# Softmax denominators of a dilated attention: summed over steps on GpSimd and over keys once a head on TensorE, output inverted and scaled in place

## What is computed

```python
def _dilated_pattern(qh, kh, vh, window, dilation):
    ...
    s = jnp.einsum('brnikge,brnjke->brnkgij', qs, kk)
    ...
    m = jnp.max(s, axis=-1)
    pexp = jnp.exp(s - m[..., None])
    l = jnp.sum(pexp, axis=-1)
    o = jnp.einsum('brnkgij,brnjke->brnikge', pexp, vv)

def dilated_attention(q, k, v, q_g, k_g):
    ...
    res = [_dilated_pattern(qh, kh, vh, w, d) for (w, d) in DILATED_PATTERNS]
    m_max = jnp.max(jnp.stack([r[1] for r in res]), axis=0)
    wts = [jnp.exp(r[1] - m_max) for r in res]
    num = sum(wi[..., None] * r[0] for wi, r in zip(wts, res))
    den = sum(wi * r[2] for wi, r in zip(wts, res))
    out = num / den[..., None]
```

## Time and profile before the change

| | us |
|---|---|
| median of 3 runs (3523.31 to 3527.47) | 3525.03 |
| the profiled execution | 3533.12 |
| its span, first to last instruction | 3531.4 |
| from the start of the mixers' transfers to the last store of that phase, about | 766 to 1408 |

### The profile page before, as it was taken

How to read it: one execution, slowest core, us unless ns; L and a number is a source line. 1 busy time by engine, 2 the same in 40 slices (tenths; PEclk the granted TensorE clock), 3 DMA queues, 4 the chain that set the end, 5 groups by cost and what they waited for, 6 DMA issues and landing times. The chain is left out here.

```text
span 3531.4 us, 38277 instructions
## 1 busy us (share of the span) xinstructions
PE 3181.3 (90%) x15558; PEld 2484.2 (70%) x15620; DVE 1606.5 (45%) x1490; ACT 813.0 (23%) x1136; POOL 329.4 (9%) x224
## 2 busy tenths in 40 slices
PE   5899999947989878799789999999998899997699
PEld 4678888824555545678568888888887787886587
DVE  5771145536466433532454444444444422422343
ACT  4221111112333433300221111111110421321331
POOL 4000000012333322000210000000000000000100
PEclk8899999968999989899889999999999999998899
DMA  3132222155385560642301111111111643532342
GB/s 120 66 130 67 71 69 73 59 141 152 98 211 139 147 156 32 197 147 97 132 36 48 48 48 48 48 48 48 48 48 37 233 165 108 194 122 81 125 133 67
DMA packets 222781, 356.21 MB, mean 101 GB/s; under 512 B 36993, under 2 KB 122241, under 8 KB 212417
## 3 DMA queue, kind: packets, MB, share of 16 engines
q1 hardware_dynamic: 218674, 333.71, 29.8%
q0 software_dynamic: 4000, 21.01, 1.6%
HBM read 257.45 MB, written 97.17 MB: 100 GB/s over the span
## 5 line engine op out<-in xcount | busy, mean ns | idle before, releaser
L78 PE MATMUL up_ps<-up_h_hi,up_w_hi 128*128 128x512 f32 x1408 | 555.7, 395 | 35.7 <-DVE up_h_lo L184 34.9
L79 PE MATMUL up_ps<-up_h_lo,up_w_hi 128*128 128x512 f32 x1408 | 553.0, 393 | 0.0
L80 PE MATMUL up_ps<-up_h_hi,up_w_lo 128*128 128x512 f32 x1408 | 552.4, 392 | 0.0
L78 PE MATMUL inp_ps<-inp_h_hi,inp_w_hi 128*128 128x512 f32 x896 | 358.5, 400 | 31.5 <-DVE inp_h_lo L184 28.7
L79 PE MATMUL inp_ps<-inp_h_lo,inp_w_hi 128*128 128x512 f32 x896 | 353.5, 394 | 0.0
L80 PE MATMUL inp_ps<-inp_h_hi,inp_w_lo 128*128 128x512 f32 x896 | 352.8, 394 | 0.0
L78 PEld LDWEIGHTS up_ps<-up_h_hi,up_w_hi 128*128 128x128 f32 x1408 | 267.3, 190 | 98.8 <-issue 32.7
L80 PEld LDWEIGHTS up_ps<-up_h_hi,up_w_lo 128*128 128x128 f32 x1408 | 267.5, 190 | 56.4
L79 PEld LDWEIGHTS up_ps<-up_h_lo,up_w_hi 128*128 128x128 f32 x1408 | 267.7, 190 | 55.7 <-issue 0.5
L78 PE MATMUL down_banks<-down_a_hi,down_w_hi 128*128 128x512 f32 x704 | 276.8, 393 | 29.5 <-DVE down_a_lo L1814 27.1
L1683 DVE TENSOR_TENSOR up_squares<-up_ps,up_rstd 128x2048 f32<-128x2048 f32 x44 | 100.9, 2292 | 440.8 <-PE up_ps L80 431.0
(11 more groups left out here) (274 smaller groups left out, 4867.0 us busy)
## 6 DMA issues: line engine op xcount, KB each, us to landing
down_a_raw<-act SPq DMA_DIRECT2D x14, 2816.0 KB, 12.2
act<-up_room SPq DMA_DIRECT2D x22, 1024.0 KB, 4.6
up_room<-in_w_up_dram SPq DMA_DIRECT2D x42, 512.0 KB, 5.9
mix_m_t<-cum_rows SPq DMA_DIRECT2D x16, 1024.0 KB, 5.5
inp_room<-in_w_in_dram SPq DMA_DIRECT2D x26, 512.0 KB, 5.0
xbc<-inp_room SPq DMA_DIRECT2D x12, 1024.0 KB, 4.6
mix_xbc<-xbc SPq DMA_DIRECT2D x16, 768.0 KB, 4.3
down_w_raw<-in_w_down_dram SPq DMA_DIRECT2D x44, 256.0 KB, 3.0
```

The lines of the kernel that those rows point to most:

```text
L78: pe.matmul(out, w_hi, x_hi, start=first, stop=False)
L79: pe.matmul(out, w_hi, x_lo, start=False, stop=False)
L80: return pe.matmul(out, w_lo, x_hi, start=False, stop=last)
```

## The change

- `values` no longer makes denominators. `add` works on half the columns; `o_den` becomes `o_sum`, outputs alone.
- GpSimd gets a new loop. For each head it clears `p_sum` (128 x 2 x 2048), and after each exponential adds that step's probabilities into the columns of `p_sum` that belong to their query tokens: dense for dilation 1, every 4th column for dilation 4, every 16th for dilation 16. Each add waits for the one before it. ScalarE may write a buffer of `probs` only when values and GpSimd are both done with what it held.
- After the last step, `sums` on TensorE multiplies `p_sum` by a tile of ones 64 wide, four blocks of 512 columns, each for two query heads side by side, into the four banks. It waits for all adds of GpSimd and VectorE. So each denominator stands on all 64 rows of its head's outputs. ScalarE copies each bank over the first half of `p_sum`.
- `divide` on VectorE inverts each block of 512 columns in place and multiplies `o_sum` by it. The store of `o_sum` follows when all four blocks are done (`sync_out`). The trip of the denominators through DRAM is gone, as are `den_rows` and its use in `out_projection`.
- The planned times: steps at k / (STEPS + 11), 8 units more between (2,2) and (2,3), the mixer's chunk at 26.4 units for 26.0. The next head's second loads stand right behind the last step.
- Waits that are new: the first pass of heads 2 and 3 and the second pass of heads 1 to 3 wait for ScalarE's copies of the sums of the head before; GpSimd's memset waits for the division of the head before.
- The row maxima are folded on 32 partitions of 128 columns, in 12 small transfers instead of 6.

```diff
     def in_step(self, r, k):
-        return self.at(2, r, k / (self.STEPS + 3))
+        return self.at(2, r, k / (self.STEPS + 11))
...
-            at += long[which - 1]
+            at += long[which - 1] + (8.0 if (which, r) == (2, KVH - 2) else 0.0)
...
-        def store(r):
-            sp.wait_ge(self.o_add, self.VALUES * (r + 1))
-            for n in range(4):
-                sp.dma_start(self.den_parts[r][n:n + 1, :], self.o_den[32 * n:32 * n + 1, 1, :]).then_inc(self.den_st, 16)
-            sp.dma_start(self.mix_t[r * P:(r + 1) * P, :], self.o_den[:, 0, :]).then_inc(self.o_st, 16)
-            sp.wait_ge(self.den_st, 64 * (r + 1))
...
-            sp.dma_start(self.den_fold[:, :, :], self.den_parts[r].rearrange("(a e) (c s) -> (e c) a s", a=2, s=32)
-                         ).then_inc(self.den_in, 16)
...
+            yield self.at(2, r, 1.0) + 9.0
+            sp.wait_ge(self.o_out, NB * (r + 1))
+            sp.dma_start(self.mix_t[r * P:(r + 1) * P, :], self.o_sum[:, :]).then_inc(self.o_st, 16)
...
+        for r in range(KVH):
+            yield self.in_step(r, 0.2)
+            if r > 0:
+                pool.wait_ge(self.o_out, NB * r)
+            else:
+                pool.wait_ge(self.built, 11)
+            pool.memset(self.p_sum[:, :, :], 0.0).then_inc(self.p_add, 1)
+            for k in range(self.STEPS):
+                g = r * self.STEPS + k
+                yield self.in_step(r, k + 1.2)
+                p, col, follows = self.step(k)
+                pool.wait_ge(self.exp_s, g + 1)
+                pool.wait_ge(self.p_add, r * (self.STEPS + 1) + k + 1)
+                new = self.probs[:, g % self.RING]
+                if p < 2:
+                    blocks = 2 if follows else 1
+                    into = self.p_sum[:, :, self.run(p, col, blocks)]
+                    new = new[:, :, 0:blocks].rearrange("p h b t -> p h (b t)")
+                else:
+                    into = self.p_sum[:, :, :].rearrange("p h (t i) -> p h i t", i=16)[:, :, col:col + 2]
+                pool.tensor_tensor(into, new, into, ALU.add).then_inc(self.p_add, 1)
...
                 if g >= self.RING:
                     act.wait_ge(self.pv_mm, self.readers(g - self.RING))
+                    act.wait_ge(self.p_add, (g - self.RING) // self.STEPS + g - self.RING + 2)
...
+            for n in range(NB):
+                yield self.in_step(r, self.STEPS + 5 + 1.5 * n)
+                act.wait_ge(self.den_mm, r * NB + n + 1)
+                act.activation(self.p_sum[:, 0, n * 512:(n + 1) * 512], self.banks[:, n], ACT.Copy).then_inc(self.den_out, 1)
...
+                yield self.at(2, r, 1.0) + 2.0 * n
+                d = r * NB + n
+                blk = slice(n * 512, (n + 1) * 512)
+                dve.wait_ge(self.den_out, d + 1)
+                dve.reciprocal(self.p_sum[:, 0, blk], self.p_sum[:, 0, blk]).then_inc(self.inverted, 1)
+                dve.wait_ge(self.inverted, d + 1)
+                dve.tensor_tensor(self.o_sum[:, blk], self.o_sum[:, blk], self.p_sum[:, 0, blk], ALU.mult).then_inc(self.o_out, 1)
...
-            for e in range(2):
-                pe.matmul(bank[cur[e], den_first], self.ones[:, :], probs[1][:, e, 0], start=True, stop=True)
...
-                last = pe.matmul(bank[cur[e], den_both], self.ones[:, :], probs[2][:, e].rearrange("p b t -> p (b t)"), start=True, stop=True)
...
+    def sums(self, pe, r, n):
+        if n == 0:
+            pe.wait_ge(self.p_add, (r + 1) * (self.STEPS + 1))
+            pe.wait_ge(self.o_add, self.VALUES * (r + 1))
+        for e in range(2):
+            last = pe.matmul(self.banks[HD * e:HD * e + HD, n], self.ones[:, :], self.p_sum[:, e, n * 512:(n + 1) * 512],
+                             start=True, stop=True)
+        last.then_inc(self.den_mm, 1)
```

132 lines of the change are left out of this document (50 added, 82 removed).

## The result

The changed kernel takes **3566.31 us** (median of 4, 3563.36 to 3571.34) against 3526.25 for the kernel before beside it: ratio 1.0114, interval 1.0097 to 1.0132. It is 40 us slower. The profiled execution took 3563.36, its span 3561.2.

What follows compares the result with a forecast made beforehand. TensorE was taken to bound the steps, VectorE the first passes of heads 2 and 3. Terms -50 + 13 + 16 + 1 + 10 - 1 - 4 gave -15, 3525 to 3510 us; range 3472 to 3565.

Steps and rivals of the forecast that it cites:

- C and E: First passes of heads 2 and 3, between step stretches; VectorE read as the limit, each about 54 us with tail.
- G: Gap before the last head's steps, where TensorE waits for queries; length set by loads after the last score, +1 us.
- Steps, -50: Four heads' softmax steps: ones-column matmuls leave TensorE, additions come to GpSimd; 351 against 401 us before.
- B, D, F and H: Softmax steps of heads 0, 1, 2 and 3; TensorE sets the pace; afterwards about 97, 87, 81 and 86 us.
- Rival 1: GpSimd's strided additions in the steps are slow, 2.05 us each: total +40, 3565 us; chance 0.25.
- Tail of a head, +13: After a head's last addition: sums and copies let the next-but-one head's first pass begin 6.5 us later; two heads, +13.
- division, +16: VectorE's reciprocals landing in C and E: 12 us each, less 4 credited for SP's freed time, +8 each.
- End, +10: After the last head's steps: sum, copy, four division blocks and store take 26 us against 16.
- Projection, -4: Output projection no longer loads 1 MB of inverses ahead of its first tile: -4 us.
- First pass, -1: Row maxima folded on 32 rows of 128: less VectorE work but six more DMA issues, -1 us.
- Rival 3: In the steps GpSimd stands in its mixer waits while probabilities pile up: +21, 3546 us; chance 0.10.
- Rival 2: GpSimd stays hidden in the steps, TensorE sets the pace everywhere: -43, 3482 us; chance 0.23.

Runs made afterwards that it cites:

- x15: x9 with the plan of before and ScalarE's mixer square moved behind the next chunk's decays; output not divided: 3435.0 us.
- x1: Changed kernel without its 16 reciprocals on VectorE, the multiplication kept: 3529.5 us.
- x9: Changed kernel without additions, sums over keys, copies and reciprocals, semaphore increments in their place; clearing and multiplication stay: 3505.4 us.
- x13: x4 with the plan of before, the sums and copies still right behind a head's last step: 3578.9 us.
- x14: Changed kernel with inverse by logarithm and exponential on ScalarE, mixer square late, last head's loads earlier, and the plan of before: 3507.1 us.
- x5: Changed kernel with the edits of x1 and x4 together: 3526.7 us.
- x4: Changed kernel, complete, with ScalarE's copies of the sums right behind a head's last exponential, ahead of the mixer's work: 3567.2 us.
- x7: Changed kernel, additions and sums kept, but divided as before: rows through DRAM, 32 columns inverted a head, the projection multiplies: 3540.3 us.
- x2: Changed kernel without GpSimd's 160 additions, semaphore increments in their place, output divided by a constant: 3548.5 us.
- x18: x16 without the 160 additions, semaphore increments in their place, sums taken over ones: 3451.4 us.
- x12: Kernel before, complete, with only ScalarE's mixer square moved behind the next chunk's decays: 3491.0 us.
- x17: x16 with the 160 additions of probabilities on VectorE in place of GpSimd: 3490.1 us.
- x16: x7 with copies of the sums first, the mixer square late and the plan of before: 3504.5 us.
- x8: x4 with the inverse made on ScalarE by logarithm and exponential, VectorE only multiplying: 3538.2 us.

## Why the prediction was wrong

It said -15 (3510) and the kernel is 40 slower, just above the range: 55 us too low. 23 of them are in C and E, 17 in the steps, 10 in G and 6 at the end, with 4 the other way in the projection and the first pass. The step that failed is the hand-over between heads. The prediction took 0.45 chunks of mixer work a head out of the steps (3.5 us of TensorE each, 14 in all) and charged them nowhere; it let the first pass follow 6.5 us after the last addition, without the mixer's work that stands ahead of the copies on ScalarE; and it took a third off the reciprocals' price. The reading of the steps failed too, but it does not carry the loss: with the square late in both kernels they stand 37.8 us apart, as they stood 40 apart without.

Term by term, from exponential to exponential as in the table:

- **Steps, -50.** Measured -33; for heads 1 to 3, -35 had been given and -15 was measured. B, D, F and H were read as "TensorE sets the pace": it was busy for 89 to 95% there, but 2 or 3 times a head the exponentials it needs stood behind a square that waited for GpSimd, and behind a bunch of decays, on ScalarE. With both out of the way the kernel before does its steps in 358 us and the changed one in 315, -43. The gaps were in the trace of before, of 5 to 9 us between two exponentials, and 19.2 us of the square's wait lie in them; the prediction names ScalarE nowhere as a limit. Steps in which TensorE does set the pace are those of x15 (73.05 busy us of 74).
- **GpSimd's additions.** The price was right for dense columns (1275); strided ones took 21 to 23% more. A head's additions came to 54.6 us where 48.3 and 3.3 for waits had been put, and GpSimd's whole, 85 us in a head's steps, had been predicted at 82 to 87. Rival 1, "slow strided additions", gave the time that was measured, 3565, but not its cause, so that is luck: its price of 2.05 us is off, and dense additions save about 6 us, not clear of none. Its threshold of 1.5 us was crossed without deciding anything.
- **Tail of a head, +13, and division, +16.** Measured +52 in C and E together. Reciprocals carry 26 of it (x1), where +16 had been given: SP's freed time was credited against them, and no run shows such a credit. The other 26 are there without any reciprocal, addition or sum (x9, +25). Two things stay in x9. One is the mixer's work that the new plan put behind the last step: in C it is 126 matmuls, where it was 84 before, and 40 instructions of ScalarE for 25. The plan of before takes 13 us off C and E in x13 and 21 in x14. The other is the wait for ScalarE's place in order, 20.7 us in x9. Taking that wait away alone gave 4 us (x5 against x1), since TensorE then waits for the mixer. With both gone, and the square late, nothing is left (x15, 93.6 us for 94.0); how the 26 divide is not shown. The tail itself took 14.2 us from first sum to first pass and not 6.5, yet cutting it alone gave nothing (x4).
- **G, +1.** Measured +11. That the loads are "ordered a little earlier in the queue" was wrong in time: two mixer loads and four value loads stood ahead of them on SP, and they went out at 1293.08, 9 us behind the last score. TensorE's wait for the queries, 20.3 in the earlier trace rows, is only 6.2, so the rest is the mixer's work in the gap, for which the plan has its 8 units more: 68 matmuls, 12 before. G is 37.0 without the new work (x9), and 26.9 and 27.9 with the old plan (x13, x15).
- **End, +10.** Measured +16, of which the reciprocals are 12 (x1). The sums, copies and the mixer's square stood between the last addition and the first reciprocal, 7.4 us where 2 had been allowed:

```profile
1418.24 3.51 PE L1019 MATMUL mix_a_banks<-mix_p_sum,mix_a_ones 128*64 128x512 f32 x8 [1.17 <-POOL mix_p_sum L774]
...
1425.59 3.34 DVE L872 RECIPROCAL mix_p_sum<-mix_p_sum 128x512 f32<-128x512 f32 x1
...
1441.66 0.34 SPq L733 DMA_DIRECT2D mix_t<-mix_o_sum  x1
```

- **Projection, -4.** Measured -6.6, and 9 when the old division is put back (x7): right in sign, low in size.
- **First pass, -1.** Measured -2.

Rival 3 (GpSimd in its mixer waits while probabilities pile up) did not happen: ScalarE waited 5.7 us for buffers. Rival 2 (GpSimd hidden) is excluded by x2 for the changed kernel (18 us) and by x18 for the freed one (53). What was right: GpSimd at 90 to 92% in the steps, VectorE the full engine in C and E (44.04 of 50 us in C), and the reciprocals as the danger there. Exponentials that wait for GpSimd, named as a sign of the forecast, came only four times, 5.7 us.

The account of the change in the kernels with the square late is short: all that the change takes out (the small products, half of the columns of VectorE's adds, the denominators' way through DRAM, their products in the projection, 7 us) costs 56 us (x12 against x15, which keeps 16 multiplications); sums over keys and the old division cost 16 (x18 against x15), additions 53 on GpSimd or 39 on VectorE. 16 + 53 is more than 56, 16 + 39 is the same. In neither form does the first half of the change beat the kernel before with its square late. The best time is 3490 to 3491, by x12 or x17; x12 is the simpler.

What stays open: how much of x16's steps is GpSimd's busy time and how much its place in the order; how much of the late square's 36 us is the square and how much the decays; how C and E's 26 us divide between plan and order; and whether additions split between the two engines would do better, which was not tried.

## What to carry to other kernels

Work taken off a busy engine is worth what the next limit leaves: before counting matmuls as won, look in the same stretch for an in-order wait on the engine that feeds it, even one that is mostly idle, and try moving that first (here a late square, with the decays that it freed, was worth 36 us, and the whole change cost 40). A long total of waits is not yet a loss: look where they lie and what stands behind them (19.2 of 133.5 us here). Price a stretch of planned work that is vacated together with the one where it lands. A step that costs 18 us when it is removed from a kernel with other limits may cost 53 when these are gone, so cost a suspect again after every fix.

## What the hardware showed

- **VectorE and GpSimd slow each other when both read from SBUF.** In x17 VectorE's additions of two SBUF tiles of 512 columns took 681 ns (673 to 695, 30 of them) if dense and 1110 (42) if strided while GpSimd did nothing; with a GpSimd instruction beside them they took 1.8 us on average, and up to 2820 and 2880 ns. GpSimd's products of 1024 columns went from 2362 ns to 2666. In the changed kernel VectorE's product of two SBUF tiles, 687 ns in the earlier trace rows, took up to 2324 (first row below; the second is GpSimd's product in x17):

```profile
L874 DVE TENSOR_TENSOR mix_o_sum<-mix_o_sum,mix_p_sum x16: 691/693/2324, 979.9 to 1440.9; 128x512 f32<-128x512 f32 x16
```

```profile
L1193 POOL TENSOR_TENSOR mix_y<-mix_y,mix_e_cum 128x1024 f32<-128x1024 f32 x16 | 42.7, 2666 | 140.9 <-DVE mix_e_cum L1335 140.9
```

  The excess, up to 2820 - 681 = 2139 ns for a dense addition, stays under one GpSimd product (2362). The Trainium skill, "SBUF — State Buffer", section "SBUF: two separate sides", says that the two engines share a pair of ports as an exclusive lock held for a whole instruction, which a VectorE operation with two SBUF inputs takes against GpSimd; the rows agree. VectorE's maxima and its sums with one operand in PSUM kept their 1217 and 686 ns in x17, which fits a lock for two SBUF inputs only.
- A change of function on ScalarE took 1.28 us each time, and in x8 both the logarithm and the exponential behind it needed one, two a head.
- A reciprocal of 512 columns took 3342 ns on VectorE at every place, 4.9 times a product.
- TensorE's granted clock was 1.00 in the steps of x15, where it was busy 73.05 of 74 us, and 0.89 to 0.92 in the steps of the changed kernel (872 to 965, 1032 to 1126, 1195 to 1290, 1322 to 1418), where it was busy for 83 to 88% of the time; in C after the change it was 0.80, against 0.91 in the earlier trace rows.
